# The output product of a hybrid encoder layer as three products of rounded parts and remainders

## What is computed

```python
for l in range(DEPTH):                      # DEPTH = 2
    # hybrid_mixer: three token mixers on h, each widened to 1024 and gated
    y = (gates[:, :, 0] * (o_diff @ w_br[0])
         + gates[:, :, 1] * (o_dsa @ w_br[1])
         + gates[:, :, 2] * (o_fox @ w_br[2]))
    m = y @ w_o                             # the output product, (512, 1024) @ (1024, 1024)
    h = layer_norm(DEEPNORM_ALPHA * h + m, ln1_g[l], ln1_b[l])
    f = grouped_moe(h, w_router, b_router, w_gate[l], w_up[l], w_down[l])
    h = layer_norm(DEEPNORM_ALPHA * h + f, ln2_g[l], ln2_b[l])
```

## Time and profile before

| what | value |
|---|---|
| median of 3 runs | 2408.04 us (2403.69 to 2410.15) |
| the profiled execution's own time | 2402.85 us |
| its span, first to last instruction | 2401.1 us |
| PE busy | 2073.7 us, 86% of the span |
| DVE busy | 906.6 us, 38% |
| ACT busy | 538.2 us, 22% |
| mean granted PE clock | 0.954 |
| moved between memory and the core | 546.09 MB, mean 227 GB/s |

### The profile page before, as it was taken

One profiled execution on the slowest core, in us unless ns is written; L12 is line 12 of the kernel. 1 busy time (PEld: TensorE's weight loads), 2 busy tenths in 40 slices (PEclk: granted clock), 3 DMA queues, 4 the chain that ended last, 5 costly groups with the idle time before them and its releaser, 6 DMA issues.

```text
span 2401.1 us, 28663 instructions
## 1 busy us (share of the span) xinstructions
PE 2073.7 (86%) x9562; PEld 1161.4 (48%) x9570; DVE 906.6 (38%) x1771; ACT 538.2 (22%) x1159; POOL 196.2 (8%) x237
## 2 busy tenths in 40 slices
PE   4999998999979988888579999999999699778883
PEld 3776676676433322223257657757764333222231
DVE  5765644444351111111268565445443411011114
ACT  2344145135000000000123432532430000000000
POOL 0000001000011111111100000010000111111111
PEclk9999999999979999999879999999999799999996
DMA  5311321231459999999832114214142799999995
GB/s 179 106 71 36 115 97 36 93 119 61 177 241 387 425 425 426 426 425 425 320 123 99 42 46 130 71 36 140 71 158 96 306 424 426 425 427 426 425 425 209
DMA packets 97947, 546.09 MB, mean 227 GB/s; under 512 B 18032, under 2 KB 20848, under 8 KB 73216
## 3 DMA queue, kind: packets, MB, share of 16 engines
q1 hardware_dynamic: 77632, 508.95, 52.3%
q0 software_dynamic: 12864, 25.21, 2.8%
q10 hardware_dynamic: 7296, 9.97, 1.7%
HBM read 528.85 MB, written 23.07 MB: 230 GB/s over the span
## 4 chain that ended last, share of the span: by engine, by line
PE 59%; DMA 20%; DVE 10%; issue 6%; ACT 2%; ACTq 1%; POOL 1%; DVEq 0%; SPq 0%; another core or an unknown queue 0%; POOLq 0%
PE ps L924 12%; PE ps L652 7%; PE ps L654 7%; PE ps L653 7%; PE ps L940 6%; DMA ring<-in_w_up 5%; PE ps L838 5%; PE ps L852 5%; DMA h<-in_w_up 4%; DMA xslot<-in_w_up 4%; PE ps L754 2%; DMA scr<-scr 2%; DMA scr<-in_w_up 2%; PE ps L805 2%; PE ps L776 2%
## 5 line engine op out<-in xcount | busy, mean ns | idle before, releaser
L652 PE MATMUL ps<-hT_lo,w_hi 128*128 128x512 f32 (+1 forms) x832 | 339.3, 408 | 22.2 <-DVE w_lo L1317 14.3
L1771 DVE COPY scr<-ps 128x512 f32<-128x512 f32 x66 | 45.7, 692 | 788.8 <-PE ps L916 788.7
L654 PE MATMUL ps<-hT_hi,w_hi 128*128 128x512 f32 (+1 forms) x832 | 327.0, 393 | 0.0
L653 PE MATMUL ps<-hT_hi,w_lo 128*128 128x512 f32 (+1 forms) x832 | 326.2, 392 | 0.0
L1055 ACT ACTIVATE scr<-ps 128x512 f32<-128x512 f32 (+3 forms) x334 | 152.1, 456 | 409.0 <-PE ps L940 307.0
L1075 ACT ACTIVATE w_hi<-ring 128x1024 fp32r<-128x1024 f32 x124 | 130.5, 1053 | 393.2 <-PE ps L654 320.9
L924 PE MATMUL ps<-ring,scr 128*64 128x512 f32 x384 | 179.0, 621 | 26.1 <-issue 14.4
L1317 DVE TENSOR_TENSOR w_lo<-ring,w_hi 128x1024 fp32r<-128x1024 f32 x124 | 150.7, 1216 | 103.3 <-ACT w_hi L1075 96.9
L652 PEld LDWEIGHTS ps<-hT_lo,w_hi 128*128 128x128 f32 (+1 forms) x832 | 156.8, 188 | 63.6 <-issue 14.6
L925 PE MATMUL ps<-ring,scr 128*64 128x512 f32 x384 | 181.2, 628 | 0.0
L838 PE MATMUL ps<-scr,ring 128*128 128x512 f32 x384 | 171.0, 607 | 3.3 <-ACT scr L1055 3.3
(11 more groups left out here) (229 smaller groups left out, 2946.4 us busy)
## 6 DMA issues: line engine op xcount, KB each, us to landing
ring<-in_w_in SPq DMA_DIRECT2D x30, 2048.0 KB, 8.0
ring<-in_w_up SPq DMA_DIRECT2D x24, 2048.0 KB, 45.1
ring<-in_w_down SPq DMA_DIRECT2D x24, 2048.0 KB, 42.6
ring<-in_w_gate SPq DMA_DIRECT2D x24, 2048.0 KB, 46.5
scr<-in_w_down SPq DMA_DIRECT2D x20, 2048.0 KB, 41.8
scr<-in_w_gate SPq DMA_DIRECT2D x18, 2048.0 KB, 46.3
scr<-in_w_up SPq DMA_DIRECT2D x14, 2048.0 KB, 47.7
xslot<-in_w_gate SPq DMA_DIRECT2D x12, 2048.0 KB, 43.5
```

Source lines behind the costliest of these rows:

```text
L652: mm(out, a[0], b[1], start=first, stop=False)
L653: mm(out, a[1], b[0], start=False, stop=False)
L654: return mm(out, a[0], b[0], start=False, stop=last)
```

## The change

The output product is computed as the projections are, from split rows and split weights.

- DVE's sum for branch "s" becomes `last_sum`: the sum of a chunk goes to one of two buffers `y_sum`, ACT copies it to the rounded part `y_hi[:, c]` (where yT was), and DVE subtracts into `y_lo[:, c]` (place 6).
- ACT's new `output_parts`, after the gates of branch "s", copies each of eight row blocks of w_o to a rounded part `wo_hi(k)`: blocks 0 to 3 in place 5 (`hT_lo`), blocks 4 to 7 in place 7 (`w_hi`, `w_lo`). DVE subtracts it from the weight in place (`wo_lo(k)` lies where the weight lay). ACT's order is weight 0, then row c and weight c + 1.
- PE's `output` makes three fp32r products instead of one f32 product. Only in its first bank it waits, block by block, for weight remainder k and row remainder k.
- Places 5, 6 and 7 can take pieces only after the last bank of the output product. So the order of the places is changed: pieces 0 and 1 go to places 0 and 3, pieces 2 to 4 to places 6, 7 and 5.

The new lines are compute and waits only; the loads are the same 96 per layer.

```diff
@@ expert_slot
-            return (6, 7, 5, 0, MRING, 1, 2, 9, 8, 4, H_SLOT)[piece_no[e, m] % XRING]
+            return (0, MRING, 6, 7, 5, 1, 2, 9, 8, 4, H_SLOT)[piece_no[e, m] % XRING]
@@ sync
                     for n in range(XRING):
-                        if n == 0:
-                            multiplied(("o", "s", NSTEP - 1))
-                        elif n < 3:
-                            multiplied(("g", "s", KD - 1))
-                        elif expert_slot(*PIECES[n]) < MRING:
+                        if expert_slot(*PIECES[n]) < MRING:
                             released([p_ for p_ in pieces if in_slot[p_] == expert_slot(*PIECES[n])][-1])
                         elif expert_slot(*PIECES[n]) == MRING:
-                            sp.wait_ge(y_ready.sem, y_ready.at("y", l))
+                            sp.wait_ge(y_summed.sem, y_summed.at(KD - 1, l))
                             alone(sp)
...
-                        elif expert_slot(*PIECES[n]) > 7:
+                        elif expert_slot(*PIECES[n]) == 4:
+                            multiplied("router")
+                        else:
                             multiplied(("m", NT - 1, 1))
-                        else:
-                            multiplied("router")
@@ tensor, output
-                    pe.wait_ge(y_ready.sem, y_ready.at("y", l))
-                    landed("wo0", l)
-                    landed("wo1", l)
...
-                                w = cols(in_slot["wo0" if k < KB else "wo1"], KB)
-                                ins = mm(bank[b].t, yT[:, k, tok(t)], w[:, k % KB, half * 512:(half + 1) * 512],
-                                         start=(k == 0), stop=(k == KD - 1))
+                                if t == 0 and half == 0:
+                                    pe.wait_ge(wo_ready.sem, wo_ready.at(k, l))
+                                    alone(pe)
+                                    pe.wait_ge(y_ready.sem, y_ready.at(("y", k), l))
+                                    alone(pe)
+                                at = slice(half * 512, (half + 1) * 512)
+                                ins = split_product(bank[b].t, (y_hi[:, k, tok(t)], y_lo[:, k, tok(t)]),
+                                                    (wo_hi(k)[:, at], wo_lo(k)[:, at]), k == 0, k == KD - 1)
@@ scalar
+                def output_parts(l):
+                    def round_weight(k):
+                        name = "wo0" if k < KB else "wo1"
+                        act.wait_ge(land[in_slot[name]].sem, land[in_slot[name]].at(name, l))
+                        nc.scalar.activation(wo_hi(k), wo_raw(k), ACT.Copy).then_inc(
+                            wo_rounded.sem, wo_rounded.tick(k))
+                    round_weight(0)
+                    for c in range(KD):
+                        act.wait_ge(y_summed.sem, y_summed.at(c, l))
+                        nc.scalar.activation(y_hi[:, c, :], y_sum[c % 2], ACT.Copy).then_inc(
+                            y_rounded.sem, y_rounded.tick(c))
+                        if c + 1 < KD:
+                            round_weight(c + 1)
@@ vector
+                def last_sum(br, l):
+                    def low(c):
+                        dve.wait_ge(y_rounded.sem, y_rounded.at(c, l))
+                        V.tensor_tensor(y_lo[:, c, :], y_sum[c % 2], y_hi[:, c, :].bitcast(F32),
+                                        ALU.subtract).then_inc(y_ready.sem, y_ready.tick(("y", c)))
+                    def low_weight(k):
+                        dve.wait_ge(wo_rounded.sem, wo_rounded.at(k, l))
+                        V.tensor_tensor(wo_lo(k), wo_raw(k), wo_hi(k).bitcast(F32), ALU.subtract).then_inc(
+                            wo_ready.sem, wo_ready.tick(k))
+                    for c in range(KD):
+                        b = c % 4
+                        dve.wait_ge(gate_ready.sem, gate_ready.at((br, c), l))
+                        filled(b, ("br", br, c), l)
+                        V.tensor_tensor(prod, gate[:, c, :], bank[b].t, ALU.mult).then_inc(bank[b].read, 1)
+                        if c >= 2:
+                            dve.wait_ge(y_ready.sem, y_ready.at(("y", c - 2), l))
+                        in_sbuf(b, ("br", br, c), l)
+                        V.tensor_tensor(y_sum[c % 2], yT[:, c, :], prod, ALU.add).then_inc(
+                            y_summed.sem, y_summed.tick(c))
+                        if c:
+                            low(c - 1)
+                        low_weight(c)
+                        dve.wait_ge(y_summed.sem, y_summed.now(l))
+                    low(KD - 1)
```

More of the change, by code:

```diff
@@ L174, in trunk @@
         w_hi, w_lo = sb("w_hi", [P, 2, UNIT], F32R), sb("w_lo", [P, 2, UNIT], F32R)
+        with nc.sbuf_tensor("ring_r", [P, RING, PIECE], F32R) as ring_r:
+            pass
         ring = sb("ring", [P, RING, PIECE])
@@ L201, in trunk @@
         rstd = sb("rstd", [P, NT])
+        with nc.sbuf_tensor("scr_r", [P, 18176], F32R) as scr_r:
+            pass
         scr = sb("scr", [P, 18176])
@@ L217, in trunk @@
         prod = scr[:, 13312:13824]
+        y_sum = [scr[:, 12288:12800], scr[:, 12800:13312]]
+        y_hi = scr_r[:, 6144:10240].rearrange("p (b t) -> p b t", t=T)
+        y_lo = scr_r[:, 0:4096].rearrange("p (b t) -> p b t", t=T)
         ptb = scr[:, 14336:16384].rearrange("p (n w) -> p n w", n=2)
@@ L322, in trunk @@
         gate_ready = signal("gate_ready")
+        y_summed = signal("y_summed")
+        y_rounded = signal("y_rounded")
+        wo_rounded = signal("wo_rounded")
+        wo_ready = signal("wo_ready")
         aff_ready = signal("aff_ready")
@@ L384, in unit_part, with wo_raw, wo_lo, wo_hi @@
             return part[:, unit_no[name, q] % 2, 0:k * c].rearrange("p (k c) -> p k c", c=c)
+        def wo_raw(k):
+            return cols(in_slot["wo0" if k < KB else "wo1"], KB)[:, k % KB, :]
+        def wo_lo(k):
+            s = in_slot["wo0" if k < KB else "wo1"]
+            return ring_r[:, s, (k % KB) * D:(k % KB + 1) * D]
+        def wo_hi(k):
+            if k < KB:
+                return hT_lo[:, 2 * k:2 * k + 2, :].rearrange("p k t -> p (k t)")
+            return (w_hi, w_lo)[(k - KB) // 2][:, k % 2, :]
         def unit_end(name, q):
@@ L1233, in _ @@
                         gates(br_, l)
+                    output_parts(l)
                     for t in range(NT):
@@ L1764, in _ @@
                         attention(br_, l)
-                        gated_sum(br_, l)
+                        if br_ == BRANCHES[-1]:
+                            last_sum(br_, l)
+                        else:
+                            gated_sum(br_, l)
                     layer_norm("ln1", l, mixer_rows(l))
```

## The result

| what | before | after |
|---|---|---|
| first comparison, median | 2407.64 us (4 runs, 2403.69 to 2410.15) | 2384.16 us (4 runs, 2384.04 to 2386.73) |
| ratio of the two, 95% interval | | 0.9906 [0.9889, 0.9924] |
| profiled execution, its span | 2402.85, 2401.1 us | 2384.22, 2382.4 us |
| PE busy | 2073.7 us | 2053.4 us |
| DVE busy | 906.6 us | 933.6 us |

The change is faster, by more than was forecast: 2384.2 us lies under the range of 2388 to 2404. The two profiled executions stand 18.6 us apart, where the forecast had 13.7.

The account below looks back on a forecast made before the run. Expert weight transfers at 425 GB/s bound the expert stages, the mixer chain the time before; -12.9 + 14.8 less 8.2 and 9.3 gave -6.3 and -7.4, together -13.7 us: 2394.3 us from 2408.04, range 2388 to 2404.

Parts of the forecast that it names:

- The base: Whole kernel: the forecast was added to the median 2408.04 us, 5.2 above the profiled execution's 2402.85.
- The dip: Early expert stage: transfers run at about half rate until places return; filling this gives back 8.2 and 9.3 us.
- The traffic: Behind the output product: three more expert pieces wait for its end, adding 3 x 4.93 = 14.8 us per layer.
- The product: Output product: three rounded products, records 0.227 us apart, replace one f32 product; 46.2 us with turns against 57.7.
- The start: Output product begins at 623.1 without waiting for the last chunk's sum, 1.7 us gained; last remainder ready at 627.7.
- Rival 1: Expert stages: first gathers stand behind a deeper queue, the half-rate stretch stays, +1.9 us per layer, 2411.8 us; chance 0.13.
- Rival 2: Output product: the clock falls, likeliest in the first bank, records 0.43 us apart, about 2472 us; chance 0.05.
- Rivals 3 and 4: Output product: 3, three products no cheaper than one, 2416.7 us, chance 0.02; 4, records closer than in a projection, 0.01.

Follow-up runs that it names:

- order_only: Kernel before with only the changed order of places and their waits, output product still in f32: 2414.62 us, ratio 1.0046.
- place6_early: Changed kernel with the rows' remainders kept elsewhere, so two pieces instead of three wait for the product's end: 2375.55 us, ratio to the kernel before 0.9892.
- five_early: place6_early in the old order with early waits, no piece held back, weights' remainders left out of the result: 2376.51 us, ratio 0.9895.
- dve_extra: Changed kernel with one more VectorE operation on 128x512 in each chunk of the last branch's sum: 2401.03 us.
- late_start: Changed kernel with one wait for all chunks ahead of the output product, in place of a wait ahead of each chunk: 2400.41 us.

## Why the prediction was wrong

The direction, the mechanism and the order of the terms held; the time lay 10.1 us under the forecast, outside the range. Of these, 5.2 us are the base. The other 4.9 are the distance of the two profiled executions, 18.6 us, from the forecast 13.7: -2.7 for the dip, -1.5 for a gather, -3.0 between the expert stages, against +1.6 for the product and +0.6 for a later start. Two steps of the prediction failed in its own terms, the base and the size of the dip; the gather and the stretch between the stages it had at nothing, and they fell its way by luck.

**The base: 5.2 us, the largest part.** The step "on the median 2408.04, which lies 5.2 above it, 2394.3" carried the error of three runs into the number. 38 further runs have medians of 2401.5 and 2403.3. In the first comparison the changed kernel's runs were centred on its profiled one, so the 5.2 us fell away.

**The dip: 2.7 us.** The step "17 x (1 - 221/425) = 8.2 us and 19 x (1 - 218/425) = 9.3 us" under-sized it. In windows of 10 us counted from the product's end it is 9.6 us in layer 1 (above) and, with 143, 321 and 390 GB/s, 9.9 us in layer 2; from the shifts of the last gate product, 14.8 - 5.2 = 9.6 and 14.8 - 4.2 = 10.6 in after, 9.6 and 9.8 in order_only. That is 1.4 and 1.3 us more than 8.2 and 9.3. I had seen the edge and put "some 1 us per layer" only into the lower bound. The larger figure rests on these rows; the times of place6_early and five_early don't decide it.

**The traffic: as priced.** 3 x 4.93 = 14.8 us a layer stands: the fourth and fifth held-back pieces together cost 9.7 us in layer 1 and 10.7 in layer 2, for 9.9.

**The product: 1.6 us the other way.** The step "Three cost 0.68" took the projection's 0.227; the records came 0.233 apart, 64 x 0.700 = 44.8 instead of 43.6, outside even the 0.231 of the bound. The reason given for 0.227, that all operands are resident, doesn't hold as a rule. The 0.3 us put down for the waits came as 0.4, lost behind the first record; that the waits cause it is not shown. With the turns the product took 47.9 us for 46.5. It began 27.14 us behind the branch's first product instead of 27.7, which gives 0.6 back. So 12.1 in place of 12.9 per layer. The Trainium skill, page "TensorE: Matmul & The Clock Gate", gives 215.7 ns between starts at 512 columns and full clock, section "Wait — 56ns, not 53.3ns?"; no row here comes that close, with 227 and 233.

**The start: right, the clock time by luck.** TensorE starts without a wait, as forecast. That 623.12 was measured for 623.1 is a coincidence: the branch began 0.57 us later than before, and the product 0.56 us sooner behind it. Remainder 7 was forecast for 627.7 and measured at 627.54. It was nearly as tight as stated, with 0.9 us to spare for the forecast 0.2; dve_extra shows what the rest costs.

**The last gather: 1.5 us, not foreseen.** Before, in layer 1, the last gather whose rows TensorE turns is issued behind the two transfers that spread the next norm's parameters, and TensorE waits for it:

```profile
1144.40 0.60 POOL L1841 DMA_DIRECT2D scr<-in_ln_g  x1
1145.00 0.57 POOL L1841 DMA_DIRECT2D scr<-in_ln_b  x1
1145.88 1.06 POOL L1851 DMA_INDIRECT scr<-h_rows,scr  x1 [0.30 <-issue]
```

```profile
1167.80 0.63 PE L916 MATMUL ps<-cf,scr 128*128 128x128 f32 x4 [1.51 <-DMA scr<-h_rows,scr]
```

It took 21.9 us from issue to use, where the earlier trace rows has 9.9 from issue to landing in the median; the two transfers ahead of it have medians of 12.3 and 18.4. After, the same gather goes out 23.2 us ahead of its use, and the wait is gone in layer 1; order_only, with 21.5 us, still waits 1.08 us. That the two transfers delay it is read from the traces; no run moved them.

**Between the expert stages: 3.0 us, not foreseen.** Code there is the same in both kernels. Before the first rows of layer 2 are turned, TensorE waits for VectorE, before 20.54 and after 19.45 us:

```profile
1198.30 1.97 PE L642 MATMUL ps<-cf,h 128*128 128x128 f32 x8 [20.54 <-DVE h L1364]
```

```profile
1189.35 1.97 PE L664 MATMUL ps<-cf,h 128*128 128x128 f32 x8 [19.45 <-DVE h L1406]
```

Some 1.7 us more come between the second and third branch's weights, and there lies a stretch at the lower clock level, from 410 us behind the experts' end, that was longer before than after (the first row is before, the second after):

```profile
1590.00:1610.00 20.00, 17.29 (x41) 8.35 (x42) 3.96 (x8) 9.35 (x19) 1.78 (x5) 0.74 0.00 0
```

```profile
1570.00:1590.00 20.00, 15.42 (x70) 10.21 (x70) 7.37 (x20) 10.71 (x34) 4.16 (x10) 0.83 0.11 43
```

The changed kernel's second profiled run has 675.33 us between the stages and order_only 686.16, 10.8 apart, against 12.1 for the product alone and 15.1 in the first pair. So this part is scatter, and a lucky one for the first pair.

**The rivals.** Rival 1, the dip stays: no, every window from +20 has 415 GB/s or more. Rival 2, the clock falls in the output: not in the changed kernel (1.00 from 620 to 670), but late_start and dve_extra show its mechanism alive: behind a pause of 4.01 us in the one, behind 3.22 and 1.72 us close together in the other. Rivals 3 and 4: no.

**The range** was too narrow below: it held the dip's edges and the scatter of three runs, but not the base's own error, the 3 us between the stages and the gather together.

## What to carry to other kernels

A stage that streams weights is described by two numbers, the bytes left at its start and the time its engines idle in it; before moving a load behind that start, measure the idle time with its edges, in windows that go on until the rate is full again. Loads that only fill it cost nothing that could be seen here, and those beyond it cost their whole length. And a forecast that is a sum over one profiled execution should stay with that execution: the median of three runs is no better a base when the runs spread over 6 us.

## What the runs showed of the hardware

- A pause of TensorE of 4.01 us in full work is followed by seven and six records at the lower clock level (0.43 us apart against 0.233), in layers 1 and 2; the 1.69 us pause of the earlier trace rows was not (there the clock stayed at 1.00). The pause's length alone doesn't decide it: in dve_extra one of 3.22 us is followed by the full pace in layer 1 (starts at 631.83, 632.14, 632.37) and by the lower level in layer 2 (1811.87, 1812.44, 1812.86).
- Records of rounded products of 512 columns come in two steady paces at full clock, 0.2267 us in the projections and 0.2333 in the output product. Projections written to banks 4 to 7 keep 0.2267, so the PSUM bank is not the cause.
- Eleven runs of one kernel spread over 5 to 14 us (2398.64 to 2403.19 for dve_extra, 2397.75 to 2412.2 for the kernel before). In the runs of the kernel before the longest has a lower mean granted clock than a short one: 2397.9 us at 0.955, 2410.4 at 0.950.
